# Second attention layer of an encoder step: V's high and low part side by side in one stationary tile, P weighted by its row sums before it is transposed

## What is computed

```python
def _fox_attend(q, k, v, cq, ck, q_pos, k_pos):
    s = jnp.einsum('bqhd,bkhd->bhqk', q, k, preferred_element_type=jnp.float32) * (FOX_HEAD_DIM ** -0.5)
    s = s + jnp.transpose(cq, (0, 2, 1))[:, :, :, None] - jnp.transpose(ck, (0, 2, 1))[:, :, None, :]
    allowed = k_pos[None, :] <= q_pos[:, None]
    p = jax.nn.softmax(jnp.where(allowed[None, None], s, -jnp.inf), axis=-1)
    return jnp.einsum('bhqk,bkhd->bqhd', p.astype(v.dtype), v)
```

## Time and profile before

| | |
|---|---|
| runs | 1498.9, 1500.3, 1500.26 us; median 1500.26 |
| profiled execution | 1503.03 us, its span 1501.2 us |
| TensorE matmul | 1470.4 us busy, 98% |
| TensorE weight load | 1424.9 us, 95%, beside the matmuls |
| VectorE | 590.4 us, 39% |
| ScalarE | 612.6 us, 41% |
| GpSimd | 445.7 us, 30% |
| mean granted TensorE clock | 0.994 of full |

### The profile page before, as it was taken

How to read it: one execution, slowest core, us unless ns; L and a number is a source line. 1 busy time by engine, 2 the same in 40 slices (tenths; PEclk the granted TensorE clock), 3 DMA queues, 4 the chain that set the end, 5 groups by cost and what they waited for, 6 DMA issues and landing times.

```text
span 1501.2 us, 28219 instructions
## 1 busy us (share of the span) xinstructions
PE 1470.4 (98%) x10923; PEld 1424.9 (95%) x10923; DVE 590.4 (39%) x1045; ACT 612.6 (41%) x1043; POOL 445.7 (30%) x220
## 2 busy tenths in 40 slices
PE   7999999999999999999999999999999999999997
PEld 7899999999999999999989999999999999999997
DVE  6788777441111111111356666663511111111113
ACT  5566666442222222222346766663522222222121
POOL 0000001344444444333400000013344444444332
PEclk9999999999999999999999999999999999999999
DMA  5333333222222222222332333321222222222222
GB/s 191 120 90 111 100 107 92 71 71 84 84 83 76 80 83 81 92 77 77 126 93 86 86 102 110 100 82 58 84 73 81 84 84 84 84 80 78 81 88 88
DMA packets 48619, 135.09 MB, mean 90 GB/s; under 512 B 6480, under 2 KB 13136, under 8 KB 48544
## 3 DMA queue, kind: packets, MB, share of 16 engines
q1 hardware_dynamic: 48544, 134.06, 29.3%
HBM read 111.22 MB, written 11.83 MB: 82 GB/s over the span
## 4 chain that ended last, share of the span: by engine, by line
PE 88%; ACT 4%; DVE 4%; issue 2%; DMA 1%; POOL 1%; SPq 0%; ACTq 0%; DVEq 0%
PE ps L585 75%; PE ops L748 3%; PE tps L700 2%; PE sps L659 2%; PE ps L626 1%; ACT w_hi L956 1%; PE ops L736 1%; DVE ol L1614 1%; PE sps L677 1%; PE sps L662 1%; DVE w_lo L1479 1%; PE sps L683 1%; POOL w_lo L1349 0%; DVE nmax L1553 0%; PE ops L755 0%
## 5 line engine op out<-in xcount | busy, mean ns | idle before, releaser
L1349 POOL TENSOR_TENSOR w_lo<-w_raw,w_hi 128x1024 fp32r<-128x1024 f32 (+1 forms) x159 | 374.0, 2353 | 1026.6 <-ACT w_hi L956 1025.2
L585 PE MATMUL ps<-xh,w_hi 128*128 128x288 f32 x2160 | 476.6, 302 | 9.6 <-issue 4.4
L585 PE MATMUL ps<-xh,w_lo 128*128 128x288 f32 x2160 | 464.2, 297 | 0.0
L585 PE MATMUL ps<-xl,w_hi 128*128 128x288 f32 x2160 | 463.6, 296 | 0.0
L956 ACT ACTIVATE w_hi<-w_raw 128x1024 fp32r<-128x1024 f32 (+1 forms) x199 | 207.5, 1043 | 448.0 <-PE ps L585 445.1
L585 PEld LDWEIGHTS ps<-xh,w_hi 128*128 128x128 f32 x2160 | 346.5, 190 | 12.0 <-issue 11.0
L585 PEld LDWEIGHTS ps<-xh,w_lo 128*128 128x128 f32 x2160 | 349.2, 189 | 0.0
L585 PEld LDWEIGHTS ps<-xl,w_hi 128*128 128x128 f32 x2160 | 348.6, 189 | 0.0
L585 PE MATMUL ps<-hh,w_hi 128*128 128x288 f32 x660 | 140.9, 294 | 0.0
L585 PE MATMUL ps<-hh,w_lo 128*128 128x288 f32 x660 | 140.8, 294 | 0.0
L585 PE MATMUL ps<-hl,w_hi 128*128 128x288 f32 x660 | 140.3, 293 | 0.0
(11 more groups left out here) (213 smaller groups left out, 1738.4 us busy)
## 6 DMA issues: line engine op xcount, KB each, us to landing
w_raw<-w_units SPq DMA_DIRECT2D x184, 512.0 KB, 3.5
w_raw<-w_units SPq DMA_DIRECT2D x16, 384.0 KB, 3.0
qsw<-qsin SPq DMA_DIRECT2D x64, 72.0 KB, 2.1
ka<-ka SPq DMA_DIRECT2D x16, 224.0 KB, 5.1
xT<-x_in SPq DMA_DIRECT2D x8, 288.0 KB, 5.9
dk_out<-kf SPq DMA_DIRECT2D x8, 288.0 KB, 3.3
dv_out<-vf SPq DMA_DIRECT2D x8, 288.0 KB, 2.2
fk_out<-kf SPq DMA_DIRECT2D x8, 288.0 KB, 2.2
```

The source lines that it names most:

```text
L585: mm = nc.tensor.matmul(out[:, half, :], w[:, k, :], rhs[:, kt, half * HALF:(half + 1) * HALF], start=start and w is w_hi[slot] and rhs is ...
L1349: nc.gpsimd.tensor_tensor(w_lo[slot][:, 0:kts, :], w_raw[slot][:, 0:kts, :], w_hi[slot][:, 0:kts, :].bitcast(F32), ALU.subtract).then_inc( ...
```

## The change

- `vh2` and `vl2` become one tile `vv` of four strips: head 0's high part, head 0's low part, head 1's low part, head 1's high part. There are no more strips of ones and zeros, and GpSimd's two memsets of them go.
- `pv_prompt` in layer 2 is two matmuls per key block, `vv` with P's high and with P's low part: 8 and not 12. One half of the output's rows is the product with V's high part, the other the one with its low part. `pv_sample` is three matmuls of 128 columns and not six.
- Since no product makes the row sums, `exps` takes them with the exponential (`accum_out`), VectorE makes the reciprocal (`share`), and the rows are multiplied by it before the transposition: jobs 0 to 4 on VectorE (`share`), jobs 5 to 9 on ScalarE (`weigh`). A transposition now waits for that (`p_ready`, `p_act`) and not for the exponential.
- After a product, ScalarE copies the other half across (`move_sample`, `move_prompt`) and VectorE adds (`join_o`). The logarithms and exponentials go.
- The tables of layer 2 have other numbers, so other steps change places too.

The core of the diff:

```diff
-F_SCORE, F_MAX, F_EXP = (3, 4, 5, 7, 7, 13, 13, 15, 18, 18), (1, 5, 5, 9, 9, 12, 14, 15, 18, 18), (1, 5, 6, 9, 9, 14, 15, 15, 18, 19)
...
+F_SCORE, F_MAX, F_EXP = (3, 5, 5, 8, 11, 11, 13, 15, 17, 19), (3, 5, 7, 8, 10, 12, 14, 15, 17, 19), (4, 5, 7, 8, 11, 12, 14, 15, 17, 20)
...
+F_SHARE, F_WEIGH = (4, 7, 8, 9, 11, 13, 15, 16, 18, 20), (6, 6, 8, 9, 9, 13, 15, 16, 18, 20)
+WEIGH_ACT = (0, 0, 0, 0, 0, 1, 1, 1, 1, 1)
...
-        vh2 = place("vh2", [P, 7, 4, 64], F32R)
-        vl2 = place("vl2", [P, 7, 4, 64], F32R)
+        vv = place("vv", [P, 7, 4, 64], F32R)
...
+                elif WEIGH_ACT[tt]:
+                    pe.wait_ge(p_act, a.c * sum(WEIGH_ACT) + sum(WEIGH_ACT[:tt + 1]))
                 else:
-                    pe.wait_ge(exp_done, val(a * 10 + (10 * G + tt + 1)))
+                    pe.wait_ge(p_ready, 5 * G + a.c * (10 - sum(WEIGH_ACT)) + tt + 1 - sum(WEIGH_ACT[:tt + 1]))
...
+                    for b in range(3):
+                        mm = nc.tensor.matmul(ops[:, 0:2 * NEW], head_cols(4 + b, h), pts[:, b, :], start=b == 0, stop=b == 2)
+                    mm.then_inc(pvs_done, 1)
+                    return
...
-                    for v, p in ((hi, pth), (hi, ptl), (lo, pth)):
...
+                    for v, p in ((vh, pth), (vh, ptl), (vl, pth)) if L == DIFF else ((vv, pth), (vv, ptl)):
...
+            def weigh(a, par, jj):
+
+                w, tau, slot = width(JOBS[FOX][jj][0]), 10 * a + jj, (10 * par + jj) % 4
+                act.wait_ge(rden_done, 10 * G + tau + 1)
+                nc.scalar.activation(pr[:, slot, 0:w], pr[:, slot, 0:w], ACT.Copy, scale=rden[:, slot:slot + 1]
+                                     ).then_inc(p_act, 1)
...
-                nc.scalar.activation(rec[r, 0:SEQ], ops[o, :], ACT.Ln).then_inc(den_logs, 1)
-                act.wait_ge(den_logs, 2 * i + 2)
-                nc.scalar.activation(rec[r, :], rec[r, :], ACT.Exp, scale=-1.0).then_inc(rec_done, 1)
...
+                nc.scalar.activation(rec[r, 0:SEQ], ops[o, :], ACT.Copy).then_inc(rec_done, 1)
...
+            def share(a, par, jj):
+
+                w, tau, slot = width(JOBS[FOX][jj][0]), 10 * a + jj, (10 * par + jj) % 4
+                dve.wait_ge(exp_done, 10 * G + tau + 1)
+                if WEIGH_ACT[(jj - 4) % 10] and tau >= 4:
+                    dve.wait_ge(p_act, (tau - 4) // 10 * sum(WEIGH_ACT) + sum(WEIGH_ACT[:(jj - 4) % 10 + 1]))
+                nc.vector.reciprocal(rden[:, slot:slot + 1], den[:, slot:slot + 1]).then_inc(rden_done, 1)
+                if not WEIGH_ACT[jj]:
+                    dve.wait_ge(rden_done, 10 * G + tau + 1)
+                    nc.vector.tensor_scalar(pr[:, slot, 0:w], pr[:, slot, 0:w], rden[:, slot:slot + 1], None, ALU.mult
+                                            ).then_inc(p_ready, 1)
```

More of the change, by code:

```diff
@@ L357, in encoder @@
         fox_set = sem("fox_set")
-        den_logs = sem("den_logs")
+        os_moved = sem("os_moved")
+        p_act = sem("p_act")
         rec_done = sem("rec_done")
@@ L726, in pv_sample @@
                         pe.wait_ge(o_scaled, val(a * 2 + h))
-                    if a.c == 0 and h == 0:
-                        pe.wait_ge(fox_set, 4)
-                elif later(a):
+                    for b in range(3):
+                        mm = nc.tensor.matmul(ops[:, 0:2 * NEW], head_cols(4 + b, h), pts[:, b, :], start=b == 0, stop=b == 2)
+                    mm.then_inc(pvs_done, 1)
+                    return
+                if later(a):
                     pe.wait_ge(oln_done, val(a))
-                hi, lo = (vh, vl) if L == DIFF else (vh2, vl2)
-                wide, narrow = (hi, 2 * NEW), (lo, NEW)
+                wide, narrow = (vh, 2 * NEW), (vl, NEW)
                 for b, blk, terms in ((0, 4, (wide, narrow)), (1, 5, (wide, narrow)), (2, 6, (narrow, wide))):
                     for v, n in terms:
-                        w = v[:, blk, :] if L == DIFF else head_cols(v, blk, h)
-                        mm = nc.tensor.matmul(ops[:, 0:n], w, pts[:, b, 0:n],
-                                              start=b == 0 and v is hi, stop=b == 2 and v is hi)
+                        mm = nc.tensor.matmul(ops[:, 0:n], v[:, blk, :], pts[:, b, 0:n],
+                                              start=b == 0 and v is vh, stop=b == 2 and v is vh)
                 mm.then_inc(pvs_done, 1)
@@ L743, in pv_prompt @@
                 pe.wait_ge(os_taken, val(v_index(L, a, h) + 1))
[L744 removed]
                 for j in range(4):
[L746 to L749 removed]
+                    for v, p in ((vh, pth), (vh, ptl), (vl, pth)) if L == DIFF else ((vv, pth), (vv, ptl)):
+                        w = v[:, j, :] if L == DIFF else head_cols(j, h)
+                        mm = nc.tensor.matmul(ops[:, P * j:SEQ], w, p[:, j, P * j:SEQ], start=j == 0 and v is not vl and p is pth,
+                                              stop=j == 3 and (v is vl or v is vv and p is ptl))
                 mm.then_inc(pvp_done, 1)
@@ L1219, in fox_attention @@
                             exps(FOX, n, par, jj)
+                    for jj in range(10):
+                        if s == F_WEIGH[jj] and WEIGH_ACT[jj]:
+                            weigh(a, par, jj)
                     if s == F_TAKE_V:
@@ L1362, in fox_layer @@
                 pool.wait_ge(acc_done, 3 * KT)
-                for tile, value in ((vh2[:, :, 1:3, :], 1.0), (vl2[:, :, 1:3, :], 0.0)):
-                    nc.gpsimd.memset(tile.bitcast(F32), value).then_inc(fox_set, 2)
-                pool.wait_ge(fox_set, 4)
-                nc.gpsimd.memset(kb[64:128, 0, :].bitcast(F32), 1.0).then_inc(fox_set, 1)
+                pool.wait_ge(f_lo_done, 1)
+                nc.gpsimd.memset(kb[64:128, 0, :].bitcast(F32), 1.0).then_inc(fox_set, 5)
                 pool.wait_ge(fox_set, 5)
@@ L1702, in fox_attention @@
                             row_max(FOX, n, par, jj)
+                    for jj in range(10):
+                        if s == F_SHARE[jj]:
+                            share(a, par, jj)
                     if s == F_V_LO:
```

77 lines of the change are left out of this document (38 added, 39 removed).

## The result

The changed kernel takes **1510.8 us** (median of 4 runs, 1510.14 to 1511.24), the one before 1500.28 us. The ratio is 1.0072, with a 95% interval of 1.0060 to 1.0084: it is slower, by 10.5 us. The forecast was 1492 us, with a range of 1484 to 1500. Sign and range were wrong. The profiled execution took 1511.24 us and its span is 1509.4 us, 8.2 us more than before, where 8.2 us less was forecast. So 16.4 us have to be found.

The account below looks back on a forecast made before the run. TensorE, busy 98% of the span, was taken as the bound. Terms -14.2 - 4.3 + 4.8 + 2.4 + 3.1 = -8.2 us, from 1503.03 us to 1494.8, or 1492 against the median of 1500.26; range 1484 to 1500.

Parts of the forecast that it names:

- the price of the weighing on VectorE: Second layer's groups: five multiplications by a column per group on VectorE, 0.45 us each on average, or 0.65 us.
- the total fits, and the order of the queues decides: Second layer's groups: VectorE and ScalarE both 78 to 80% busy of a 31 us group, so their added work fits.
- Rival 3: Second layer's groups: slower, the chain through a group closes on itself at ScalarE's queue; 33.6 us groups, 1512 us; chance 0.10.
- Matmuls removed: Second layer's value products: 0.62 us off the prompt's, 0.27 off the sample's, 16 times, 14.2 us removed (10 to 16).
- Waits that go: TensorE's waits for V's and P's low parts, 0.35 and 0.27 us per group, vanish: 4.3 us over seven groups.
- The wait that comes: Between transpositions 6 and 7, TensorE waits for the shared PSUM tile: 0.6 us, 8 times, 4.8 us.
- The other margins of 0.1 to 0.25 us: At transpositions 1, 2, 3, 6 and 8, rows weighed first; 0.3 us per group allowed, 2.4 us.
- Work added: Per group of the second layer: VectorE +3.3 us (up to +4.3), to 24.7; ScalarE from 22.0 to 24.2 us.
- The head: Start of the second layer: group 0's second score matmul 3.1 us later, through ScalarE's and SyncE's orders; 1.5 to 6.
- The clock: At the second layer's head: a longer idle stretch may prolong or move the 1.2 GHz level, within 1.5 to 6 us.

## Why the prediction was wrong

- **The step that failed** is the price of the weighing on VectorE: 0.45 us on average, 0.65 at most, from rows in which GpSimd was idle, and with it "the total fits, and the order of the queues decides". The 512, 384 and 128 wide ones kept to it (489, 421 and 288 ns). The 128x256 one cost 2.56 us, seven times, since it meets GpSimd's instruction. With what hangs on it (1.77 us of idle TensorE per group, the low clock in three) it is 18.3 of the 18.8 us between the forecast and the result. (By the profiled executions, of which the one of before was 2.8 us above its median, the miss is 16.4 us and the hold 18.6.) The bounds of the weighing and of the waits were built from the engines' own durations, and GpSimd appears in no term and in no rival, although counts 8 of its instructions in the stretch. Rival 3 gave 1512 us, near the result, but that is luck: no chain closed on itself and ScalarE was never full. Its group of 33.6 us, which looks like the 33.55 measured, does not even follow from its own terms (33.1 - 1.8 - 0.6 + 3.4 is 34.1).
- **The rest of the sum was about right.** Without the hold the kernel takes 1492.53 us, and the forecast was 1492. Its parts, by group: 33.24 before and 31.60 after is -1.64 us, where -14.2 - 4.3 + 4.8 + 2.4 over eight groups was -1.4. That the totals agree to within 1 us is partly luck. With the sizes that the traces show, given in the points below, the sum is -15.7 - 3.2 + 7.2 + 0 + 3.8 = -7.9 us, where it was -14.2 - 4.3 + 4.8 + 2.4 + 3.1 = -8.2: single terms are off by up to 2.4 us and cancel.
- **Matmuls removed**: the prompt product fell from 1.85 to 1.24 us, as said. The sample's product was priced at 0.27 us and lost 0.37 on average; from its first matmul to the next instruction it took 0.69 and 0.71 us, and 0.29 and 0.37 with GpSimd later. That makes 16 x 0.98 = 15.7 us. But a matmul taken away did not shorten the run by its whole length, as the prediction had it: the third product, put back, costs 6.8 of the 9.9 us. The rows with GpSimd later:

```profile
858.39 0.44 PE L733 MATMUL ops<-pts,vv 128*128 128x128 f32 x3
858.68 0.48 PE L588 MATMUL ps<-xh,w_hi 128*128 128x288 f32 x2
```

- **Waits that go**: V's low part, yes. P's low part before the second head's value product, only in part: 0.16 of the 0.27 us stay. That is 7 x 0.46 = 3.2 us of the 4.3 in the sum.
- **The wait that comes**: at the right place, mis-sized: 0.90 us and not 0.6. The hand walk had seen the move in ScalarE's queue (0.2 us) and not that it starts only when the write of Q's part ahead of it ends. The other margins of 0.1 to 0.25 us held in most cases, so that the 2.4 us allowed for them were not used.
- **Work added**: VectorE's 3.3 us per group do not follow from their terms (ten times 0.156 and five times 0.45 us are 3.8). Measured without the hold, it went from 21.6 to 24.3 us per group, and ScalarE from 22.1 to 23.9, so the error did no harm.
- **The head**: 3.8 us and not 3.1, released by `kb` as said; ScalarE's order was worth 2.6 of it, and not the "1 us later" of the prediction, because TensorE's slots resume later (an idle stretch of 3.89 us for 1.82). The prediction took that to lie inside the wait for the copies. With the copies swapped, no copy is waited for, and the matmul is late all the same.
- **The clock**: the prediction spoke of it only at the head. There the granted clock from 760 to 787 us is 0.87 in both kernels. What it cost lay in the groups, behind the idle stretch of 1.77 us, 4.7 us in all.

## What to carry to other kernels

Before a VectorE instruction that has all its data in SBUF is put into a schedule, look at what GpSimd does in that stretch: the engines' busy shares did not show it here, and where the two met, VectorE's instruction took as long as GpSimd's. The cure was a wait on the engine that has slack (18.3 us), or, in part, shorter instructions on it (11.2 us). And where one engine has three short steps to do between two of TensorE's, a new order may only choose which of them is waited for: here it helped only after one of them had been taken away.

## What was not expected of the hardware

- A 128x256 fp32 multiplication by a column takes 0.354 us alone and 2.56 us when it starts 0.04 us *before* a GpSimd instruction of 2.37 us. It ends 0.15 us after GpSimd's; with half the columns on GpSimd it takes 1.48 us.
- GpSimd can be the one that waits. The trace of before already had a sign of it: its instruction at 1000.05 took 2.69 us and not 2.40, begun while VectorE was at `kb` from two tensors in SBUF (999.38, 1.09 us).
- The same idle stretch of 1.77 us on TensorE, in the same place of every group, is followed by the 1.2 GHz level in only three of seven groups of the changed kernel, in two of seven with the copies swapped, and in none with ScalarE's order at the head back as well. Where no idle stretch is over 0.9 us (the two halves, and GpSimd later) the granted clock in the groups is 1.00. One stretch costs 1.55 us.
- Matmuls put back into a stretch in which TensorE is busy for 97% of the time cost 0.81 us per group for 1.28 us of their own time, because the wait behind them is shorter by 0.3 us; the rest is not accounted for.
